# A transformer-and-scan kernel on one NeuronCore: the mixers' projections in matmuls of 256 columns where they were of 512

## The chip, the core and the metric

The kernel runs on one core of one Trainium2 chip. The metric is the time of one execution on the device in microseconds (us). The kernel before takes 1607.89 us in the median of 3 runs (1607.69 to 1608.31). TensorE (PE in the profile, with its weight loads as PEld) multiplies; VectorE (DVE), ScalarE (ACT) and GpSimd (POOL) do the elementwise work; SyncE (SP) issues the loads of weights.

## The reference

256 tokens of width 1024 go through two layers of one block and then one layer of another. Each layer of the first block is a gated feed-forward network, a stage with three mixers, and a second feed-forward network. The part in question is the projection ahead of the mixers:

```
h = rms_norm(x, mix_norm[l])
aq, ak, av, bq, bk, bv, cq, ck, cv, cg, gates = jnp.split(h @ w_in[l], split_points, axis=-1)
```

The first ten pieces of `h @ w_in[l]` are 4608 columns in all: nine groups of 512. The pieces of mixer a (differential attention), b (attention over chunks with a bias table) and c (retention) are made from them; `gates` (3072 columns) scale what the mixers give.

## The kernel before

Every product of two float32 matrices is made from three products of rounded parts: with h = h_hi + h_lo and w = w_hi + w_lo, the kernel adds h_hi·w_hi, h_hi·w_lo and h_lo·w_hi in PSUM. Weights come from HBM in slabs of 128 x 2048 numbers into a ring of five slots. ScalarE writes the high part (`whi`, line 692), then VectorE the low part (`wlo`, line 1913), and only then may TensorE use the slab; TensorE's last matmul of a slab frees the slot (`used`).

Nearly all matmuls have a stationary operand of 128 x 128 and a moving one of 128 x 256. In the feed-forward networks, the gates and the output projections the weights are stationary and the activations move (`block3`, lines 1240 to 1242). In the nine groups (`group(g)`, lines 1438 to 1440) it is the other way round: the activations `h1hi`/`h1lo` (128 of the 1024 features by 128 tokens) are stationary and 512 columns of weights move, so that tokens come out on the partitions. A group takes two slabs, 8 feature blocks k, two halves of the tokens tt and three products: 48 matmuls of 512 columns, each with its own weight load. Two layers of nine groups make 864 such matmuls. tt = 0 and tt = 1 accumulate in two different banks of PSUM, and groups alternate between two pairs of banks.

The order is written out by hand. In each of the two layers TensorE does the last feed-forward products, group 0, the sums over tokens for the norm (`token_sums`, lines 1260 and 1263), groups 1, 2, 3 and 4, and then groups 5 to 8 with the transposes (line 1452) or attention scores (line 1463) of the mixers between them; after group 8 come the gates' products and the rest of the mixers. ScalarE takes each group out of PSUM (line 865). VectorE normalises and rotates the queries and keys (lines 1913, 2232) between its low parts of slabs.

Two terms of the text below: a *restart* is the first matmul of a row of projection, gate or feed-forward matmuls after a wait or after matmuls of another kind; a *train* is all that follow it without a break. The helper `settle` (line 1230) is four small matmuls of 128 x 64 that the program puts into a bank ahead of some of the trains of feed-forward and output matmuls; there is none in the projections.

Of the kernel before, what the change touches and what calls it, by code (L numbers as in the profile page):

```python
# [24 lines left out]
KT = D // P  # L25
S = 256
# [154 lines left out]
def build_program(nc, t):  # L181
# [1036 lines left out]
    def _(pe):  # L1218
        def weights(g):

            slot = PLACE[g] % NS
            pe.wait_ge(lo_done[slot], SPLITS[g])
            return slot
# [13 lines left out]
        def block3(out, slot, b, hi, lo, start, stop, skip=False):  # L1237

            w_hi, w_lo = (w[:, slot, b * P:(b + 1) * P] for w in (whi, wlo))
            pe.matmul(out, w_hi, hi, start=start, stop=False, skip_group_check=skip)  # L1240
            pe.matmul(out, w_lo, hi, start=False, stop=False, skip_group_check=skip)  # L1241
            return pe.matmul(out, w_hi, lo, start=False, stop=stop, skip_group_check=skip)  # L1242
# [11 lines left out]
        def token_sums(n, token_major):  # L1254

            bank = 6 if token_major else 7
            if n == 0:
                pe.wait_ge(first_landed, 16)
            pe.wait_ge(sq_added, n + 1)
            ins = pe.matmul(ps[:, bank, 0:S], ones[:, :], sq[:, 0, :], start=True, stop=True)  # L1260
            if token_major:
                for tt in range(ST):
                    ins = pe.matmul(ps[:, bank, S + tt:S + tt + 1], sq[:, 0, tt * P:(tt + 1) * P], ones[:, 0:1],
                                    start=True, stop=True)
            ins.then_inc(ssum_done, 1)
# [153 lines left out]
        for l in range(DEPTH):  # L1419
# [4 lines left out]
            def group(g):  # L1424

                if g >= 2:
                    pe.wait_ge(proj_evac, NGRP * l + g - 1)
                for half in range(2):
                    slot = weights(m + PROJ0 + 2 * g + half)
                    for kk in range(4):  # L1430
                        k = 4 * half + kk
                        if g == 0 and kk % 2 == 0:
                            pe.wait_ge(h_lo_ready, 4 * (n + 1) + k // 2 + 1)
                        w_hi, w_lo = (w[:, slot, kk * 512:(kk + 1) * 512] for w in (whi, wlo))
                        for tt in range(ST):
                            out = ps[:, 2 * (g % 2) + tt, :]
                            h_hi, h_lo = (h[:, k, tt * P:(tt + 1) * P] for h in (h1hi, h1lo))
                            pe.matmul(out, h_hi, w_hi, start=(k == 0), stop=False)  # L1438
                            pe.matmul(out, h_hi, w_lo, start=False, stop=False)  # L1439
                            ins = pe.matmul(out, h_lo, w_hi, start=False, stop=(k == KT - 1))  # L1440
                    ins.then_inc(used[slot], 1)
                if g == 0:
                    token_sums(n + 1, True)
# [55 lines left out]
            def values(h):  # L1499

                cols = slice(h * P, (h + 1) * P)
                pe.matmul(ps[:, 5, cols], pT[:, 3 * h, :], vA[:, 0, cols], start=True, stop=False)
                pe.matmul(ps[:, 5, cols], pT[:, 3 * h + 1, :], vA[:, 1, cols], start=False, stop=True)
                return pe.matmul(ps[:, 4, cols], pT[:, 3 * h + 2, :], vA[:, 0, cols], start=True, stop=True)

            def b_head(p):

                h = 2 * (p % 4) + p // 4
                return slice(h * HD, (h + 1) * HD)

            def y_b_out(c, par, tt):

                first = 2048 + c * S + tt * P
                return ps_flat[64 * par:64 * par + 64, first:first + P]

            for g in range(5):
                group(g)
# [3 lines left out]
            pe.wait_ge(qk_ready, 3 * l + 1)  # L1521
            transposes(TA, q_and_k(qkA, 4))
            group(5)
            stage(SA1)
            scores(SA1, S)
            group(6)
            stage(SA0)
            scores(SA0, P)
# [11 lines left out]
            for h in range(AH):  # L1540
                ins = values(h)
# [18 lines left out]
            for c in range(4):  # L1560
                for kt in range(2):
                    for par in range(2):
                        p = c + 4 * par
                        pe.matmul(y_b_out(c, par, 1), vB[:, kt, b_head(p)], pT[:, 2 * p + kt, :],
                                  start=(kt == 0), stop=(kt == 1))
# [4 lines left out]
            for c in range(4):  # L1570
                for par in range(2):
                    p = c + 4 * par
                    ins = pe.matmul(y_b_out(c, par, 0), vB[:, 0, b_head(p)], pT[:, p, :], start=True, stop=True)
# [4 lines left out]
            for j in range(2):  # L1578
                for par in range(2):
                    rows = slice(64 * par, 64 * par + 64)  # L1580
                    for kt in range(2):
                        width = S - kt * P
                        ins = pe.matmul(ps[:, 4 + 2 * par + kt, j * width:(j + 1) * width],
                                        qkT[rows, 2 + j, kt * P:(kt + 1) * P],
                                        qkT[rows, j, kt * P:S], start=True, stop=True)
# [3 lines left out]
            for h in range(CH):  # L1589
                cols = slice(h * P, (h + 1) * P)  # L1590
                pe.matmul(ps[:, 4, cols], pTC[:, h, 0, 0:P], vC[:, 0, cols], start=True, stop=True)
                for kt in range(2):
                    ins = pe.matmul(ps[:, 5, cols], pTC[:, h, kt, P:S], vC[:, kt, cols],
                                    start=(kt == 0), stop=(kt == 1))
# [11 lines left out]
            for q in range(6):  # L1606
# [12 lines left out]
                for mm in range(4):  # L1619
                    c = (1 - q % 2) * 1024 + mm * S  # L1620
                    for k in range(4):
                        kk = Y_AT["abc"[q // 2]] + k
                        ins = block3(ps_flat[:, c:c + S], slot, mm * 4 + k, yT_hi[:, kk, :], yT_lo[:, kk, :],
                                     start=(k == 0), stop=(k == 3))
# [35 lines left out]
        def state(d, g, bank, pairs):  # L1660

            for j, (lhs, rhs) in enumerate(pairs):
                ins = pe.matmul(ps[:, bank + 2 * d + g // 2, (g % 2) * S:(g % 2) * S + 192], lhs[:, g * P:(g + 1) * P],
                                rhs[:, g * 192:(g + 1) * 192], start=(j == 0), stop=(j == len(pairs) - 1))
            return ins
# [4 lines left out]
        for d in range(2):  # L1670
            for g in range(NG):
                if (d, g) == (0, 3):
                    pe.wait_ge(sq_added, NF3 + 1)
                    for j in range(2):
                        ins = pe.matmul(ps[:, 0, 0:S], ones[:, :], sq[:, j, :], start=(j == 0), stop=(j == 1))
                    ins.then_inc(sum2_done, 1)
                ins = state(d, g, 4, [(cb_tok[:, i, :], xw_c[i][:, d, :]) for i in range(2)])
# [16 lines left out]
        for j in range(1, 4):  # L1694
# [3 lines left out]
            for c in range(1, 4):  # L1698
                slot = PLACE[b2 + c // 2] % NS
                for k in (2 * j, 2 * j + 1):  # L1700
                    ins = block3(ps[:, c, 0:S], slot, (c % 2) * KT + k, hhi[:, k, :], hlo[:, k, :],
                                 start=False, stop=(k == KT - 1))
# [39 lines left out]
        for c in range(4, 23):  # L1742
            projection(c)
            if c == 4:
                pe.wait_ge(h0_ready, 1)
                for tt in range(ST):
                    ins = pe.matmul(ps[:, 7, 24 * tt:24 * tt + 24], dtT[:, tt * P:(tt + 1) * P], sel[:, 0:24],
                                    start=True, stop=True)
                ins.then_inc(dt_tok_done, 1)
            if c == 8:  # L1750
# [3 lines left out]
                for q, (lhs, rhs) in enumerate(sums):  # L1754
                    ins = pe.matmul(ps[:, 7, 128 + 12 * q:140 + 12 * q], lhs, rhs, start=True, stop=True)
# [5 lines left out]
            if c == 11:  # L1761
# [3 lines left out]
                for e, (lhs, rhs) in enumerate(sums):  # L1765
                    ins = pe.matmul(ps[0:NH, 7, e * P:(e + 1) * P], lhs, rhs, start=True, stop=True)
                ins.then_inc(sums_done, 1)
            if c == 5:
                pe.wait_ge(uz_evac, 2)
                pe.wait_ge(h0_ready, 1)  # L1770
                for tt in range(ST):
                    for ch in range(2):
                        ins = pe.matmul(ps[:, 4 + tt, ch * S:(ch + 1) * S], u_t[:, ch, tt * P:(tt + 1) * P], dft_chan[:, :, :],
                                        start=True, stop=True)
                ins.then_inc(dft_done, 1)
            if c == 7:
                pe.wait_ge(dft_evac, 1)
                for ch in range(2):
                    for tt in range(ST):
                        for part in range(2):  # L1780
                            ins = pe.matmul(ps[:, 6, ch * S:(ch + 1) * S],
                                            w1[:, tt, ch * S + part * P:ch * S + (part + 1) * P], dft_tok[:, tt, part, :],
                                            start=(tt == 0 and part == 0), stop=(tt == 1 and part == 1))
                ins.then_inc(dft_done, 1)
            if c == 20:
# [4 lines left out]
                for d in range(2):  # L1790
                    for g in range(NG):
                        ins = state(d, g, 4, [(b_tok[:, d, :], xw_x[:, d, :])])
# [30 lines left out]
        for tt in range(ST):  # L1823
            for g in range(NG):
                tok = slice(tt * P, (tt + 1) * P)
                ins = pe.matmul(ps[:, 4 + tt, g * P:(g + 1) * P], b_t[:, g, tok], c_t[:, g, tok], start=True, stop=True)
# [65 lines left out]
        for k in (0, 6, 7):  # L1892
# [4 lines left out]
            for tt in range(ST):  # L1897
                ins = pe.matmul(ps[:, 1, tt:tt + 1], sq[:, k, tt * P:(tt + 1) * P], ones[:, 0:1],
                                start=(k == 0 and tt == 0), stop=(k == 7), skip_group_check=True)
# [996 lines left out]
```

## Time and profile before

| | |
|---|---|
| median of 3 runs | 1607.89 us (1607.69 to 1608.31) |
| profiled execution | 1608.59 us |
| span of its trace | 1606.8 us |
| PE busy | 1593.5 us (99%), 13104 matmuls |
| DVE busy | 1291.6 us (80%) |
| ACT busy | 927.2 us (58%) |
| POOL busy | 211.9 us (13%) |
| 864 matmuls of 512 columns (lines 1438 to 1440) | first at 191.6 us, last at 912.1 us of the span, half of them in each layer |

Busy time is the union of an engine's instructions. A matmul's duration in the trace lasts to the end of its results, and the next one starts long before that; what counts is the distance from start to start. Such distances are read from first and last starts and the number of matmuls between them.

### The profile page before, as it was taken

The numbers are of one execution on the slowest core, as the hardware profiler recorded it, in microseconds if no ns is written. First come the engines' busy times: TensorE is split into PE (matmuls) and PEld (weight loads), VectorE is DVE, ScalarE is ACT, GpSimd is POOL, SyncE is SP. The second block draws the span as 40 slices with busy tenths as digits, with TensorE's granted clock in tenths as the row PEclk, the third lists the DMA queues.
The fourth block names the chain that finished last, engine by engine and source line by source line (L and its number), as shares of the span: only waits on it lengthen the run. The fifth ranks groups of instructions, "written<-read, shape, count | busy, mean of one in ns | idle before, by whom it ended". The sixth has DMA issues, their size and how long they took to land.

```text
span 1606.8 us, 29855 instructions
## 1 busy us (share of the span) xinstructions
PE 1593.5 (99%) x13104; PEld 1530.3 (95%) x13104; DVE 1291.6 (80%) x1468; ACT 927.2 (58%) x1113; POOL 211.9 (13%) x125
## 2 busy tenths in 40 slices
PE   9999999999999999999999999999999999999998
PEld 8999988999999999999987899999999989899998
DVE  7887978688888987897878688785899788896655
ACT  7554655685465455554565677464546567754544
POOL 1000100000040001110010000032232378600000
PEclk9999999999999999999999999999999999999999
DMA  7677654444566665766754444555554345335552
GB/s 292 226 271 270 258 188 158 158 146 170 210 217 252 251 257 202 278 243 265 282 187 160 159 155 158 177 218 206 186 207 182 135 151 190 134 132 199 195 186 77
DMA packets 48408, 320.73 MB, mean 200 GB/s; under 512 B 5388, under 2 KB 8204, under 8 KB 10776
## 3 DMA queue, kind: packets, MB, share of 16 engines
q1 hardware_dynamic: 48136, 318.81, 54.0%
q8 instruction: 103, 1.69, 0.4%
q14 instruction: 25, 0.20, 0.0%
q10 hardware_dynamic: 144, 0.02, 0.0%
HBM read 317.74 MB, written 1.07 MB: 198 GB/s over the span
## 4 chain that ended last, share of the span: by engine, by line
PE 91%; DVE 5%; ACT 2%; DMA 1%; issue 0%; SPq 0%; DVEq 0%
PE ps L1240 26%; PE ps L1242 25%; PE ps L1241 25%; PE ps L1438 3%; PE ps L1440 3%; PE ps L1439 3%; DVE wlo L1913 1%; PE ps L1452 1%; ACT whi L692 1%; PE ps L1463 1%; DMA raw<-in_w_dram 1%; PE ps L1725 1%; DVE tmp L1913 1%; DVE qkA L1913 1%; DVE pre L2550 1%
## 5 line engine op out<-in xcount | busy, mean ns | idle before, releaser
L1913 DVE TENSOR_TENSOR wlo<-raw,whi 128x2048 fp32r<-128x2048 f32 (+2 forms) x255 | 583.7, 2297 | 94.3 <-ACT whi L692 90.6
L692 ACT ACTIVATE whi<-raw 128x2048 fp32r<-128x2048 f32 (+1 forms) x264 | 499.9, 1906 | 208.3 <-DMA raw<-in_w_dram 208.0
L1240 PE MATMUL ps<-h1hi,whi 128*128 128x256 f32 x1792 | 500.6, 279 | 1.5 <-DVE wlo L1913 1.5
L1241 PE MATMUL ps<-h1hi,wlo 128*128 128x256 f32 x1792 | 496.6, 277 | 0.0
L1242 PE MATMUL ps<-h1lo,whi 128*128 128x256 f32 x1792 | 496.6, 277 | 0.0
L1240 PEld LDWEIGHTS ps<-h1hi,whi 128*128 128x128 f32 x1792 | 337.8, 189 | 5.4 <-issue 2.3
L1241 PEld LDWEIGHTS ps<-h1hi,wlo 128*128 128x128 f32 x1792 | 337.7, 188 | 0.1
L1242 PEld LDWEIGHTS ps<-h1lo,whi 128*128 128x128 f32 x1792 | 337.4, 188 | 0.0
L1240 PE MATMUL ps<-hid_hi,whi 128*128 128x256 f32 x880 | 243.8, 277 | 0.0
L1242 PE MATMUL ps<-hid_lo,whi 128*128 128x256 f32 x880 | 243.1, 276 | 0.0
L1241 PE MATMUL ps<-hid_hi,wlo 128*128 128x256 f32 x880 | 243.1, 276 | 0.0
L1240 PE MATMUL ps<-hhi,whi 128*128 128x256 f32 x672 | 190.3, 283 | 3.1 <-DVE hlo L2512 1.7
L1242 PE MATMUL ps<-hlo,whi 128*128 128x256 f32 x672 | 186.1, 277 | 0.0
L1241 PE MATMUL ps<-hhi,wlo 128*128 128x256 f32 x672 | 186.1, 277 | 0.0
L1240 PEld LDWEIGHTS ps<-hid_hi,whi 128*128 128x128 f32 x880 | 165.4, 188 | 0.2
L1241 PEld LDWEIGHTS ps<-hid_hi,wlo 128*128 128x128 f32 x880 | 165.2, 188 | 0.0
L1242 PEld LDWEIGHTS ps<-hid_lo,whi 128*128 128x128 f32 x880 | 165.2, 188 | 0.0
L585 POOL TENSOR_TENSOR sq<-sq 128x512 f32<-128x512 f32 x18 | 27.3, 1517 | 927.1 <-ACT sq L721 914.1
L1240 PEld LDWEIGHTS ps<-hhi,whi 128*128 128x128 f32 x672 | 126.4, 188 | 6.5 <-issue 3.2
L1241 PEld LDWEIGHTS ps<-hhi,wlo 128*128 128x128 f32 x672 | 126.3, 188 | 1.3 <-issue 1.2
L1242 PEld LDWEIGHTS ps<-hlo,whi 128*128 128x128 f32 x672 | 126.3, 188 | 0.0
L726 ACT ACTIVATE t_exp<-t_exp 128x512 f32<-128x512 f32 x55 | 34.7, 631 | 139.5 <-DVE t_exp L2067 139.4
(376 smaller groups left out, 2592.6 us busy)
## 6 DMA issues: line engine op xcount, KB each, us to landing
raw<-in_w_dram SPq DMA_DIRECT2D x288, 1024.0 KB, 4.8
from_start<-decay_dram SPq DMA_DIRECT2D x3, 768.0 KB, 4.5
raw<-in_w_dram SPq DMA_DIRECT2D x8, 256.0 KB, 5.8
c_rows<-in_c_rows_dram SPq DMA_DIRECT2D x2, 1024.0 KB, 10.3
relbias<-in_relbias_dram SPq DMA_DIRECT2D x2, 1024.0 KB, 7.8
pv<-in_pv_dram SPq DMA_DIRECT2D x2, 641.0 KB, 7.6
xT<-in_x_dram SPq DMA_DIRECT2D x4, 256.0 KB, 5.0
raw<-in_w_dram SPq DMA_DIRECT2D x2, 512.0 KB, 6.9
```

The costliest lines, as they stand in the source:

```text
L585: step.done(pool.tensor_tensor(sq[:, 0:2, :], sq[:, 0:2, :], sq[:, 2 * j:2 * j + 2, :], ALU.add))
L692: act.activation(whi[:, slot, c], raw[:, slot, c], ACT.Copy).then_inc(hi_done[slot], 1)
L726: step.done(act.activation(v, v, ACT.Exp, scale=-1.0))
L1240: pe.matmul(out, w_hi, hi, start=start, stop=False, skip_group_check=skip)
L1241: pe.matmul(out, w_lo, hi, start=False, stop=False, skip_group_check=skip)
L1242: return pe.matmul(out, w_hi, lo, start=False, stop=stop, skip_group_check=skip)
L1438: pe.matmul(out, h_hi, w_hi, start=(k == 0), stop=False)
L1439: pe.matmul(out, h_hi, w_lo, start=False, stop=False)
L1440: ins = pe.matmul(out, h_lo, w_hi, start=False, stop=(k == KT - 1))
L1452: ins = pe.transpose(ps_flat[:, first + j * P:first + (j + 1) * P], tile, ident[:, :])
L1463: ins = pe.matmul(ps_flat[:, c:c + width], qkT[rows, j, tt * P:(tt + 1) * P], qkT[rows, 4 + j, 0:width], start=True, stop=True)
L1913: return dve.tensor_tensor(out, a, b, op)
```

## The change

Each matmul of 512 moving columns becomes two of 256: for one half of the columns all three products, then for the other half all three. The same stationary operand is therefore loaded six times where it was three. The first matmul of a bank still clears the bank's flags, now once per bank and group, as `start` is set only for the first half.

```diff
-                            pe.matmul(out, h_hi, w_hi, start=(k == 0), stop=False)
-                            pe.matmul(out, h_hi, w_lo, start=False, stop=False)
-                            ins = pe.matmul(out, h_lo, w_hi, start=False, stop=(k == KT - 1))
+                            for n_ in range(2):
+                                c = slice(n_ * S, (n_ + 1) * S)
+                                pe.matmul(out[:, c], h_hi, w_hi[:, c], start=(k == 0 and n_ == 0), stop=False,
+                                          skip_group_check=True)
+                                pe.matmul(out[:, c], h_hi, w_lo[:, c], start=False, stop=False, skip_group_check=True)
+                                ins = pe.matmul(out[:, c], h_lo, w_hi[:, c], start=False, stop=(k == KT - 1),
+                                                skip_group_check=True)
```

The order on TensorE where layer 0 goes from the feed-forward network into group 0, before (hid: its hidden values):

```order
L1240 MATMUL ps<-hid_hi_85,whi 128x256
L1241 MATMUL ps<-hid_hi_85,wlo 128x256
L1242 MATMUL ps<-hid_lo_87,whi 128x256
L1438 MATMUL ps<-whi,h1hi 128x512
L1439 MATMUL ps<-wlo,h1hi 128x512
L1440 MATMUL ps<-whi,h1lo 128x512
```

and in the changed kernel:

```order
L1240 MATMUL ps<-hid_hi_85,whi 128x256
L1241 MATMUL ps<-hid_hi_85,wlo 128x256
L1242 MATMUL ps<-hid_lo_87,whi 128x256
L1440 MATMUL ps<-whi,h1hi 128x256
L1442 MATMUL ps<-wlo,h1hi 128x256
L1443 MATMUL ps<-whi,h1lo 128x256
L1440 MATMUL ps<-whi,h1hi 128x256
L1442 MATMUL ps<-wlo,h1hi 128x256
L1443 MATMUL ps<-whi,h1lo 128x256
```

Three matmuls of 512 have become six of 256 with the same neighbours ahead. The second place, also on TensorE, is the seam between the token sums and group 1, before:

```order
L1440 MATMUL ps<-whi,h1lo 128x512
L1260 MATMUL ps<-sq,ones 128x256
L1263 MATMUL ps<-ones,sq 128x1 x2
L1438 MATMUL ps<-whi,h1hi 128x512
L1439 MATMUL ps<-wlo,h1hi 128x512
L1440 MATMUL ps<-whi,h1lo 128x512
```

and in the changed kernel:

```order
L1443 MATMUL ps<-whi,h1lo 128x256
L1260 MATMUL ps<-sq,ones 128x256
L1263 MATMUL ps<-ones,sq 128x1 x2
L1440 MATMUL ps<-whi,h1hi 128x256
L1442 MATMUL ps<-wlo,h1hi 128x256
L1443 MATMUL ps<-whi,h1lo 128x256
```

Here too only the width and the number of the matmuls differ. No instruction of the other engines is added, removed or moved.

## Rows read from the trace of the kernel before

**Rows 1.** The page: share of the span by engine, granted clock, the last chain.
```profile
PE 1593.5 (99%) x13104; PEld 1530.3 (95%) x13104; DVE 1291.6 (80%) x1468; ACT 927.2 (58%) x1113; POOL 211.9 (13%) x125
...
PEclk9999999999999999999999999999999999999999
...
PE 91%; DVE 5%; ACT 2%; DMA 1%; issue 0%; SPq 0%; DVEq 0%
```

**Rows 2.** One line's matmuls in a stretch: duration min/median/max in ns, first and last start.
```profile
L1438 PE MATMUL ps<-whi,h1hi x47: 394/394/394, 204.2 to 235.8; 128*128 128x512 f32 x47
```

**Rows 3.** Busy us and count (x) by stretch, clock, DMA: first fast, then slow 256-column trains.
```profile
1435.00:1595.00 160.00, 160.00 (x1414) 160.00 (x1414) 99.71 (x90) 79.21 (x73) 0.00 (x0) 1.00 0.47 172
...
1164.50:1185.50 21.00, 21.00 (x181) 21.00 (x180) 19.92 (x30) 10.21 (x12) 5.87 (x2) 1.00 0.56 201
```

**Rows 4.** The same matmul line in six short trains beside or like the projections.
```profile
L1240 PE MATMUL ps<-h1hi,whi x15: 276/276/277, 311.3 to 316.1; 128*128 128x256 f32 x15
L1240 PE MATMUL ps<-h1hi,whi x15: 281/281/281, 346.3 to 351.3; 128*128 128x256 f32 x15
L1240 PE MATMUL ps<-h1hi,whi x31: 276/276/277, 374.9 to 385.1; 128*128 128x256 f32 x31
L1240 PE MATMUL ps<-h1hi,whi x15: 281/281/281, 924.3 to 929.2; 128*128 128x256 f32 x15
L1240 PE MATMUL ps<-h1hi,whi x15: 281/281/281, 1219.2 to 1224.2; 128*128 128x256 f32 x15
L1240 PE MATMUL ps<-hhi,whi x7: 281/281/281, 1291.9 to 1294.0; 128*128 128x256 f32 x7
```

**Rows 5.** PE in order of time (start, duration in us): three seams after narrow matmuls.
```profile
203.03 0.50 PE L1263 MATMUL ps<-ones,sq 128*128 128x1 f32 x4
203.39 0.48 PE L1438 MATMUL ps<-whi,h1hi 128*128 128x512 f32 x1
203.71 0.39 PE L1439 MATMUL ps<-wlo,h1hi 128*128 128x512 f32 x1
...
1218.57 0.37 PE L1322 MATMUL ps<-small,ones 128*128 128x12 f32 x2
1218.80 0.36 PE L1240 MATMUL ps<-h1hi,whi 128*128 128x256 f32 x1
```

**Rows 6.** The chain of waits, 214 to 243 us: start, us, what.
```profile
214.41 0.24 PE ps L1440
214.67 1.27 ACT qkA L865 x2
...
219.72 2.29 DVE wlo L1913
...
240.33 2.30 DVE wlo L1913
```

**Rows 7.** PE in order of time, at the two slabs of group 4.
```profile
236.22 0.40 PE L1440 MATMUL ps<-whi,h1lo 128*128 128x512 f32 x1
236.63 0.47 PE L1438 MATMUL ps<-whi,h1hi 128*128 128x512 f32 x1
236.94 0.40 PE L1439 MATMUL ps<-wlo,h1hi 128*128 128x512 f32 x1
...
241.84 0.40 PE L1439 MATMUL ps<-wlo,h1hi 128*128 128x512 f32 x1
242.08 0.39 PE L1440 MATMUL ps<-whi,h1lo 128*128 128x512 f32 x1
242.68 0.51 PE L1438 MATMUL ps<-whi,h1hi 128*128 128x512 f32 x1 [0.21 <-DVE wlo L1913]
243.02 0.40 PE L1439 MATMUL ps<-wlo,h1hi 128*128 128x512 f32 x1
```

**Rows 8.** Two long pieces of the chain of waits, 243 to 300 us.
```profile
248.47 1.75 PE ps L1452 x16
261.22 1.93 PE ps L1463 x16
```

## The prediction

> **What bounds the kernel now.** I read the page first, then the matmul lines by group, the timeline of TensorE around every restart, and last the chain of waits in the projection stage. On the page TensorE is busy for 99% of the span at the full granted clock of 2.4 GHz (tenths of 9, mean 0.999), and 91% of the chain that ended last is TensorE; no other engine is over 80% [rows 1]. So the time is the sum of start-to-start distances of some 13,000 matmuls, and a change in the distance counts nearly everywhere. The exception to look for is a place where TensorE arrives at a slab before VectorE has finished its low part.
>
> Distances. In a train (all matmuls that follow a restart without a break) of 512 columns line 1438 comes once in three, and 46 intervals take 235.8 − 204.2 = 31.6 us: 31.6 / 138 = 229.0 ns per matmul [rows 2]. The 256-column matmuls have two paces. In the last feed-forward network, 1414 matmuls touch a stretch of 160 us; about 2.4 of them only overlap its edges (each lasts 0.28 us, over two distances), which leaves 160 / 1411.6 = 113.3 ns [rows 3], its first row. In another stretch it is 21 / (181 − 2.4) = 117.6 ns [rows 3], its second; from the first and last starts of several such trains I take 117.8. The reader can tell the paces apart by the duration of one matmul: 276 ns at 113.3, 281 at 117.8, and a train keeps its pace from its restart to its end [rows 4]. The 512-column matmuls have a slow pace as well, but rarely: from 236.94 to 241.84 there are 21 distances, 233.3 ns each [rows 7]. That is one half-group of the 18 half-groups of layer 0, and layer 1 has none.
>
> **The change part by part.** It removes 864 matmuls of 512 columns and 864 weight loads, and adds 1728 of each with 256 columns. What counts is two of the new distances against one old one:
>
> - fast pace: 2 × 113.3 = 226.7 ns (from unrounded thirds of 340 ns), against 229.0: −2.3 ns per pair
> - slow pace: 2 × 117.8 = 235.6 ns: +6.6 ns per pair
>
> These are the two bounds of the unknown, from rows of the same shape in the same program, and they lie on both sides of zero. All 864 pairs fast would be −2.0 us, all slow +5.7 us, before anything is hidden. That loads and matmuls can alternate at 113.3 ns, I need not assume: the feed-forward networks do it for hundreds of us with a load for each matmul, beside VectorE at 62% [rows 3]. The operands are the other way round here (weights move), but both are 128 contiguous and 256 contiguous numbers, and the 512-column trains show no other penalty. The wait instructions, evacuations and DMAs are the same; the last matmul of a slab ends within 0.01 us of where it did. I cost these at nothing.
>
> The Trainium skill has a rule that speaks against the change. "TensorE: Matmul & The Clock Gate", section "Wait — 56ns, not 53.3ns?", gives a matmul a fixed cost of about 2.5 ns on top of N / 2.4 GHz, so 864 more of them would cost 2.2 us. The trace doesn't bear it out: by that rule the two widths would be 109 and 216 ns, and they are 113.3 and 229.0 [rows 2, 3]. The same page says nothing of two paces.
>
> Which pace does each new train get? Each layer has these trains, in matmuls of the old width:
>
> - Group 0 (48) follows the feed-forward products without a break, and these are fast; it stays fast: −0.11 us.
> - Groups 1 to 3 (144) restart after the token sums, whose last matmuls have one column [rows 5]. The nearest things in the trace are two restarts of 256 columns after matmuls of 12 and 24 columns, at 1218.8 and 1291.4; both trains are slow [rows 4, 5]. I take slow: 144 × 6.6 = +0.95 us, a third of it in group 1.
> - Group 4 (2 × 24) restarts twice after a wait for a slab.
> - Groups 5 to 8 (48 each) restart after sixteen transposes or sixteen scores [rows 8]. The gates' products restart after the same kinds: after scores fast at 311.3 and slow at 924.3, after transposes slow at 346.3 and fast at 374.9 [rows 4]. Of the 20 trains from 299 to 376 and 912 to 990 us that no `settle` precedes, I count 8 slow, and of the longer ones after transposes or scores about half. I take two of four slow: 2 × 48 × 6.6 − 2 × 48 × 2.3 = +0.41 us.
>
> What VectorE hides. At 242.68 TensorE waits for a low part [rows 7]. The chain behind it begins where group 1 ends, at 214.41: ScalarE takes group 1 out, squares it, makes a high part, and from 219.72 VectorE works nearly without a break to 242.6 [rows 6]. So group 0 and group 1 move that chain, and groups 2, 3 and 4a lie beside it. TensorE's room there: at 236.22 it waits for 236.63 − 236.22 − 0.23 = 0.18 us, and at 242.08 for 0.60 − 0.23 = 0.37 us; each wait also costs a restart, 0.31 − 0.23 = 0.08 and 0.34 − 0.23 = 0.11 us. Together 0.74 us of cover. Groups 1 to 3 slow and 4a slow (24 × (235.6 − 233.3) = 0.06) ask for 1.01 us, less 0.11 from group 0. So TensorE is late by 0.90 − 0.74 = +0.16 us at the middle of group 4, while the low part is late by 0.32 − 0.11 = 0.21 us: both come within 0.1 us of each other, and I take +0.2. If the waits vanish there is no restart, and group 4b goes on slow: 24 × 6.6 = +0.16. Had the trains been fast, the waits would only grow and the cover give back nothing but groups 0 and 1.
>
> Sum per layer: +0.2 + 0.16 + 0.41 = +0.77 us. Layer 1 has the same waits, the second 0.1 us longer, so +0.7. Together +1.5 us. The profiled execution took 1608.59 us (span 1606.8 and 1.8 around it) and would become 1610.1; it lies 0.7 us above the median of 1607.89, and so my forecast is **1609.4 us**.
>
> **The rivals.**
>
> - *All trains fast.* For it: half of the restarts in the gates are fast, and 13 of the 14 restarts of 512 columns reach their fast pace. Against it: the two slow trains after narrow matmuls. Each layer: −0.11 and −0.11 for groups 0 and 1 (2 and 3 drown in the wait for VectorE), −0.05 for 4b, −0.44 for groups 5 to 8: −0.7, both layers −1.4: 1606.5 us.
> - *All slow, and the later trains thrown anew.* This is the slower side. All of groups 5 to 8 slow gives 0.2 + 0.16 + 4 × 0.32 = 1.6 per layer, +3.2 us. It decides against the kernel when, on top, the fast trains behind the projections that no `settle` protects turn slow, since their restarts now come at other instants: the longest, from 374.5 on and its like in layer 1, have 240 matmuls each at 4.5 ns, +1.1 us apiece [rows 4]. With both: +5.4, 1613.3 us. Against it: those restarts follow the same instructions as before, and the executions of this kernel agree within 0.6 us, so the pace isn't drawn afresh in each execution.
> - *A fixed price for each matmul* (the skill's rule above): +2.2 us, 1610.1 us. Two distances of 113.3 are less than one of 229.0, so the rows leave no room for it. Little chance.
> - *No change at all.* If the cover of 0.74 us took all, and groups 5 to 8 came out even: 1607.9 us. This is the middle between the first rival and my forecast and needs no mechanism of its own.
>
> **How the numbers follow.** My forecast (trains mixed) 0.55, all fast 0.2, mostly or all slow with or without the later trains 0.17, the fixed price 0.03, anything else 0.05. A measurement of this kernel tells about 0.2% (3.2 us) from no change. The mixed case spans about 1607.5 to 1611, since each of its eight undecided groups is worth 0.43 us; with the all-fast end at 1606.5 and the all-slow end at 1611.1 the range is 1606.2 to 1612.0. Slower by over 0.2% needs the second rival nearly in full: 0.14. Faster by over 0.2% is beyond what all 864 pairs could give: 0.03. Within 0.2%: 0.83.
>
> **What would show it.** Lines 1440, 1442 and 1443 of the changed kernel: 276 ns in group 0, 281 in groups 1 to 3, and a mixture in groups 5 to 8; the wait at 236.2 gone and that at 242.1 near zero. From the start of group 0 to the gates' first product each layer should take 0.7 to 0.8 us longer. I am wrong if the new distances are neither 113.3 nor 117.8 (weights as the moving operand would then matter, or six loads of which four repeat), if groups 1 to 3 are fast, or if the difference lies outside the projections.

## The result and the profile after

The changed kernel takes 1612.86 us in the median of 7 executions, the kernel before 1608.20 us in 7 on the same chip: ratio 1.0035, 95% interval 1.0026 to 1.0044. It is slower by some 0.3%; I had forecast 1609.4 us and a range up to 1612.0, so the prediction was wrong: the time lies above the range. Two of the seven executions took 1618 us; they were not profiled, and what they had more is open. One execution of a kernel further down took 1650.04 us at a granted clock of 0.96 and is left out of that kernel's median. The profiled execution took 1612.52 us, with a span of 1610.7.

The page of the changed kernel, against [rows 1]:

```profile
PE 1598.3 (99%) x13968; PEld 1573.0 (98%) x13968; DVE 1295.7 (80%) x1468; ACT 926.9 (58%) x1113; POOL 214.3 (13%) x125
...
PEclk9999999999999999999999999999999999999999
...
PE 96%; DVE 1%; ACT 1%; DMA 0%; SPq 0%; issue 0%; DVEq 0%; ACTq 0%
```

There are 864 more matmuls, each with its load. The clock is the same. VectorE has left the chain (5% before, 1% now): it no longer sets anything in the projections, because TensorE has become later there than VectorE.

The first of the three products of the split groups, by stretch (duration min/median/max in ns, first and last start): group 0, groups 1 to 4, groups 5, 6, 7 and 8 of layer 0, and group 5 of layer 1.

```profile
L1440 PE MATMUL ps<-whi,h1hi x32: 276/276/278, 191.1 to 201.7; 128*128 128x256 f32 x32
...
L1440 PE MATMUL ps<-whi,h1hi x111: 278/280/280, 203.2 to 242.1; 128*128 128x256 f32 x111
...
L1440 PE MATMUL ps<-whi,h1hi x32: 280/280/366, 249.8 to 260.8; 128*128 128x256 f32 x32
L1440 PE MATMUL ps<-whi,h1hi x31: 279/279/387, 263.2 to 273.9; 128*128 128x256 f32 x31
L1440 PE MATMUL ps<-whi,h1hi x31: 279/279/388, 275.8 to 286.5; 128*128 128x256 f32 x31
L1440 PE MATMUL ps<-whi,h1hi x31: 279/279/363, 288.9 to 299.6; 128*128 128x256 f32 x31
...
L1440 PE MATMUL ps<-whi,h1hi x32: 279/279/365, 865.6 to 876.6; 128*128 128x256 f32 x32
```

276 ns means 113.3 ns from start to start, 279 to 281 means 117.8: in the second row 110 intervals of three matmuls take 242.1 − 203.2 = 38.9 us, 117.9 ns each. So group 0 kept the fast pace and every other train of the split groups took the slow one, ten of ten in the two layers (groups 1 to 4 are one train a layer here, groups 5, 6, 7 and 8 one each). In [rows 2] a 512-column matmul took 229.0 ns, two of the new ones now take 235.6.

At the two places where TensorE waited before [rows 7]:

```profile
235.97 0.28 PE L1443 MATMUL ps<-whi,h1lo 128*128 128x256 f32 x1
236.09 0.28 PE L1440 MATMUL ps<-whi,h1hi 128*128 128x256 f32 x1
236.21 0.28 PE L1442 MATMUL ps<-wlo,h1hi 128*128 128x256 f32 x1
...
242.33 0.28 PE L1443 MATMUL ps<-whi,h1lo 128*128 128x256 f32 x1
242.45 0.32 PE L1440 MATMUL ps<-whi,h1hi 128*128 128x256 f32 x1
242.61 0.28 PE L1442 MATMUL ps<-wlo,h1hi 128*128 128x256 f32 x1
```

The first wait is gone, and of the second a distance of 0.16 in place of 0.12 us is left.

From the first projection matmul to the first gates' matmul a layer takes 110.40 us where it took 108.84 (191.61 to 300.45 before, 191.11 to 301.51 after; layer 1 the same within 0.01 us). That is +1.56 us twice. Outside the projections one long train has changed its pace, the gates' and branches' 240 matmuls of layer 0 (line 1240, before at 276 ns in [rows 4]):

```profile
L1240 PE MATMUL ps<-h1hi,whi x29: 281/281/281, 376.0 to 385.9; 128*128 128x256 f32 x29
```

Its 240 matmuls at 4.45 ns give +1.05 us. So: 1.56 + 1.05 + 1.56 = 4.17, less 0.50 us that this execution was ahead already at 20 us of the span, plus 0.25 us at one stop (from the last matmul ahead of it to the restart 0.47 us at 1206 us of the span before, 0.72 us at 1210 us after). That makes 3.9 us; the two spans differ by 3.96. Behind that stop short trains of 24 to 54 matmuls in the second block changed their pace in both directions and about cancel. The first 20 us wait for the first loads, and between the profiles of this study they lie between 1.0 us ahead of and 0.6 us behind the kernel before; that is not the change's.

### The profile page after: what moved, and what is told of

Its sections match the earlier page's. It is cut to its first block, busy times and chain, and to the rows that moved or that the text cites. A ratio compares the mean times of both kernels' runs of the same rounds, so it can differ in the third digit from the quotient of the medians.

```text
span 1610.7 us, 31583 instructions
## 1 busy us (share of the span) xinstructions
PE 1598.3 (99%) x13968; PEld 1573.0 (98%) x13968; DVE 1295.7 (80%) x1468; ACT 926.9 (58%) x1113; POOL 214.3 (13%) x125
## 4 chain that ended last, share of the span: by engine, by line
PE 96%; DVE 1%; ACT 1%; DMA 0%; SPq 0%; issue 0%; DVEq 0%; ACTq 0%
PE ps L1240 26%; PE ps L1241 26%; PE ps L1242 26%; PE ps L1440 4%; PE ps L1442 4%; PE ps L1443 4%; PE ps L1456 1%; PE ps L1467 1%; PE ps L1729 1%; ACT whi L692 0%; DMA raw<-in_w_dram 0%; PE ps L1230 0%; DVE wlo L1917 0%; PE ps L1568 0%; PE ps L1597 0%; PE ps L1785 0%
## 5 line engine op out<-in xcount | busy, mean ns | idle before, releaser
L1440 PE MATMUL ps<-whi,h1hi 128*128 128x256 f32 x576 | 161.8, 281 | 0.0
L1442 PE MATMUL ps<-wlo,h1hi 128*128 128x256 f32 x576 | 160.7, 279 | 0.0
L1443 PE MATMUL ps<-whi,h1lo 128*128 128x256 f32 x576 | 160.6, 279 | 0.0
```

The costliest lines, as they stand in the source:

```text
L1440: pe.matmul(out[:, c], h_hi, w_hi[:, c], start=(k == 0 and n_ == 0), stop=False, skip_group_check=True)
L1442: pe.matmul(out[:, c], h_hi, w_lo[:, c], start=False, stop=False, skip_group_check=True)
L1443: ins = pe.matmul(out[:, c], h_lo, w_hi[:, c], start=False, stop=(k == KT - 1), skip_group_check=True)
```

## The experiments

The table gives each kernel's median with its ratio to the kernel before (and its 95% interval), and the length of the stage from the first projection matmul to the first gates' matmul, layer 0 / layer 1, from the profile.

| kernel | median, us | ratio | stage, us |
|---|---|---|---|
| before | 1608.0 to 1608.6 | 1 | 108.84 / 108.85 |
| changed | 1612.86 | 1.0035 (1.0026 to 1.0044) | 110.40 / 110.41 |
| changed, once more | 1612.78 | 1.0024 (1.0015 to 1.0033) | 110.40 / 110.41 |
| settle ahead of the groups | 1613.23 | 1.0031 (1.0019 to 1.0044) | 111.49 / 111.49 |
| settle ahead of gate slab 10 | 1614.28 | 1.0031 (1.0018 to 1.0045) | 110.83 / 110.40 |
| first feature block wide | 1611.09 | 1.0017 (1.0007 to 1.0027) | 109.91 / 109.91 |
| only groups 5 to 8 split | 1610.42 | 1.0013 (1.0004 to 1.0023) | 110.06 / 110.14 |
| product by product | 1614.06 | 1.0038 (1.0023 to 1.0053) | 110.40 / 110.91 |
| roles exchanged | 1612.12, one execution | | 109.60 / 109.46 |
| switches chosen | 1608.91 | 1.0002 (0.9993 to 1.0011) | 109.00 / 109.00 |
| switch after one more | 1609.48, one execution | | 109.00 / 109.00 |
| switches refitted | 1609.00 | 1.0006 (0.9989 to 1.0024) | 109.00 / 109.01 |

**The changed kernel once more.** Nothing is edited.

> The changed kernel once more. If the pace of a train belongs to the program: the same trains at 281 ns as in its first profile, all of groups 1 to 8 in both layers, and about 1612.9 us. If it is drawn anew in each execution: some of the ten trains fast.

The same ten trains were slow, the train at 376 us too, and both stages had the same length to 0.01 us. In the projections, the gates and the feed-forward networks the pace of a train belongs to the program here; it isn't drawn in each execution. That doesn't hold for every train: two short ones of the second block, of 24 and 48 matmuls, were slow in the first profile of the changed kernel and fast in this one. The longer of them, first and then second profile:

```profile
L1240 PE MATMUL ps<-hhi,whi x16: 281/281/384, 1426.4 to 1431.8; 128*128 128x256 f32 x16
...
L1240 PE MATMUL ps<-hhi,whi x16: 276/276/386, 1426.6 to 1431.8; 128*128 128x256 f32 x16
```

**Only groups 5 to 8 split.** Groups 0 to 4 keep their matmuls of 512 columns.

```diff
+                            if g < 5:
+                                pe.matmul(out, h_hi, w_hi, start=(k == 0), stop=False, skip_group_check=True)
...
+                                continue
```

> Only groups 5 to 8 are split, groups 0 to 4 keep 512 columns. Theory A with the cover by VectorE: each of the four groups costs 48 x 6.4 ns = 0.305 us, 1.22 us a layer, 2.4 us in all, and 1.05 us more if the gates' train at 375 us falls slow again: 1610.7 or 1611.7 us. If the cost of the change sat in groups 1 to 4 instead, under 1609 us.

All eight split trains were slow, and the stages 1.22 and 1.29 us longer; four times 0.305 is 1.22, and in layer 1 TensorE also stopped briefly ahead of group 0. So of the change's 1.56 us a layer, 1.22 lie in groups 5 to 8 and only 0.34 in groups 0 to 4, though those have 240 of the 432 pairs. 192 slow pairs cost 1.22 us where nothing covers them. Groups 1 to 4 would cost 1.2 us by the same price (192 × 6.4 ns); the waits for VectorE, and group 0 with its 0.1 us less, took the rest. This train of 240 matmuls at 376 us was fast again: so the price there (1.05 us) isn't a price of the split as such. Why it is paid in the changed kernel and not here wasn't found.

**Settle ahead of the groups.**

```diff
                     slot = weights(m + PROJ0 + 2 * g + half)
+                    if half == 0 and g in (1, 4, 5, 6, 7, 8):
+                        settle(2 * (g % 2))
```

> The changed kernel with the four small matmuls of settle() ahead of groups 1, 4, 5, 6, 7 and 8. Theory A (the pace is set at a restart; 117.8 ns a matmul after a bad one, 113.3 after a good one): the trains behind a settle show 276 ns a matmul in place of 281. Each group 5 to 8 then gains 95 x 4.45 ns = 0.42 us and pays about 0.19 us for the settle; groups 1 and 4 gain at most 0.2 us, as VectorE takes over. Against the changed kernel about -2.0 to -2.5 us, so about 1610.5 us; against the kernel before +2. Theory B (weights as the moving operand, or six loads with four repeats, cost 4.45 ns by themselves once the matmul is 256 wide): 281 ns stays, and the 12 settles add about 2 us: 1614.9 us.

Neither theory held in full. Groups 1 to 3, the second half of group 4 and group 5 of layer 0, in this kernel:

```profile
L1442 PE MATMUL ps<-whi,h1hi x95: 276/276/384, 203.7 to 235.7; 128*128 128x256 f32 x95
...
L1442 PE MATMUL ps<-whi,h1hi x16: 276/276/384, 242.9 to 248.1; 128*128 128x256 f32 x16
...
L1442 PE MATMUL ps<-whi,h1hi x30: 278/280/392, 250.5 to 260.9; 128*128 128x256 f32 x30
```

The train of groups 1 to 3 became fast, so weights as the moving operand do run at 113.3 ns and theory B falls. But the first half of group 4 and all of groups 5 to 8 stayed slow behind the same small matmuls, in both layers. The second half of group 4 restarted with no settle directly ahead of it and became fast, in both layers too: a restart with the weights moving can be a good one. The stage is 1.09 us longer than in the changed kernel. To the end of group 4 this kernel is 0.29 us ahead of it, two settles included; a wait for VectorE of 0.24 us ahead of group 4 takes part of the gain back. From there on the four settles ahead of groups 5 to 8, which bought nothing, make it 1.38 us longer, 0.35 us each.

**Settle ahead of gate slab 10.**

```diff
-            gate_slab(10)
+            gate_slab(10, True)
```

> The changed kernel with settle() ahead of gate slab 10, the start of the train of 240 matmuls at 375 us (layer 0) and 991 us (layer 1). In the changed kernel's profile that train is slow in layer 0 (281 ns). With the settle it should be fast in both: -1.05 us, and +0.2 us for each settle, so about 0.7 us below the changed kernel, 1612.2. If its pace has nothing to do with the excess: +0.4 us.

A miss: the train stayed slow in layer 0 and turned slow in layer 1, where it had been fast. Line 1240 in layer 0 and layer 1 of this kernel, then in layer 0 a feed-forward train behind a stop at 169.4 us, and group 0 behind that train:

```profile
L1240 PE MATMUL ps<-h1hi,whi x28: 281/281/281, 378.4 to 388.0; 128*128 128x256 f32 x28
...
L1240 PE MATMUL ps<-h1hi,whi x29: 281/281/388, 993.8 to 1003.8; 128*128 128x256 f32 x29
...
L1240 PE MATMUL ps<-h1hi,whi x32: 281/281/359, 169.7 to 180.7; 128*128 128x256 f32 x32
...
L1440 PE MATMUL ps<-whi,h1hi x32: 280/280/282, 192.4 to 203.3; 128*128 128x256 f32 x32
```

The last two rows are no part of the edit. In this one execution TensorE stopped inside a feed-forward network (0.31 us from start to start in place of 0.11; the low part of a slab ended at 169.5, so a late slab is likely). The 192 matmuls behind that kept 117.8 ns, and so did the 96 of group 0, which follow them without a stop. That is why this kernel's stage in layer 0 is 110.83 us and not 110.40. 288 times 4.45 ns are 1.28 us. The profile of the kernel with refitted switches (below) has two such trains, of 240 matmuls at 524 us and 144 at 653 us, where the other kernels are fast. Whether the executions of 1618 us had one wasn't seen.

**Product by product.**

```diff
-                            for n_ in range(2):
...
+                            for j_, (h_, w_) in enumerate(((h_hi, w_hi), (h_hi, w_lo), (h_lo, w_hi))):
+                                for n_ in range(2):
+                                    c = slice(n_ * S, (n_ + 1) * S)
+                                    ins = pe.matmul(out[:, c], h_, w_[:, c], start=(k == 0 and j_ == 0 and n_ == 0),
...
```

> All groups split, but product by product: h_hi w_hi for both halves of the columns, then h_hi w_lo for both, then h_lo w_hi for both. Theory A: the order of the six makes no difference, trains at 276 or 281 ns by their restart, total within 1 us of the changed kernel (1612.9). Theory B in the form that a repeated load of the same stationary tile costs: the same tile now comes four times in a row and then the other twice, which changes the number of changes of tile per six (two in place of four), so the pace moves away from 117.8 ns in all groups, down towards 113.3: 1609.5 us or less.

All trains from group 1 on slow at 279 to 281 ns, the stage of layer 0 the same to 0.01 us. The order of the six, and how often a tile is loaded twice in a row, makes no difference to the slow pace. In layer 1 TensorE waited once for 0.2 us for h1lo inside the seam to group 0, and so group 0 restarted and was slow too, +0.5 us: group 0 takes over the pace of what it follows without a stop, fast or slow, and a stop ends that.

**Roles exchanged.** The other two products are edited alike.

```diff
-                                pe.matmul(out[:, c], h_hi, w_hi[:, c], start=(k == 0 and n_ == 0), stop=False,
+                                pe.matmul(out[:, c], w_hi[:, 0:P], h1hi[:, k, :], start=(k == 0 and n_ == 0), stop=False,
...
```

> The changed kernel with the roles in the projections exchanged: 128 columns of the weights are stationary and 256 tokens of h move, as in the gates (the products are other ones than those wanted, the shapes and counts are the same). If weights as the moving operand make the slow pace likelier, the trains of groups 1 to 8 should now be mixed as in the gates (about 12 of 20 fast). If the restart or the place decides, the six trains of a layer stay at 281 ns.

Groups 5, 6, 7 and 8 of layer 0 and then of layer 1, the first product:

```profile
L1440 PE MATMUL ps<-h1hi,whi x28: 276/276/276, 251.0 to 260.2; 128*128 128x256 f32 x28
L1440 PE MATMUL ps<-h1hi,whi x27: 281/281/281, 264.0 to 273.2; 128*128 128x256 f32 x27
L1440 PE MATMUL ps<-h1hi,whi x28: 281/281/281, 276.3 to 285.8; 128*128 128x256 f32 x28
L1440 PE MATMUL ps<-h1hi,whi x27: 276/276/276, 290.0 to 298.9; 128*128 128x256 f32 x27
...
L1440 PE MATMUL ps<-h1hi,whi x29: 281/281/364, 866.0 to 875.9; 128*128 128x256 f32 x29
L1440 PE MATMUL ps<-h1hi,whi x27: 276/276/276, 879.8 to 888.7; 128*128 128x256 f32 x27
L1440 PE MATMUL ps<-h1hi,whi x27: 276/276/276, 892.0 to 900.8; 128*128 128x256 f32 x27
L1440 PE MATMUL ps<-h1hi,whi x29: 281/281/281, 905.0 to 914.9; 128*128 128x256 f32 x29
```

Four of eight are fast, as in the gates; groups 1 to 3 are slow in both layers. (In layer 1 the second half of group 4 and group 0, which restarted behind a short stop, were fast.) With the roles of the changed kernel the same eight places were slow in every one of its relatives: 32 of 32 in the changed kernel, the product-by-product one, the one with groups 5 to 8 and the one with the gate settled. These are eight places in four nearly equal programs and not 32 independent draws, but at the same places the roles made a difference. So the place and the neighbours alone don't decide. My tally from the gates was taken from matmuls with the other roles, and that is the likely reason why it misled; why the roles matter isn't shown.

**First feature block wide.** The first six matmuls of a train keep 512 columns.

```diff
+                            if k == 0 and g in (1, 4, 5, 6, 7, 8):
+                                pe.matmul(out, h_hi, w_hi, start=(k == 0), stop=False, skip_group_check=True)
...
+                                continue
```

> The changed kernel, but the first feature block of groups 1, 4, 5, 6, 7 and 8 (6 matmuls) keeps its 512 columns, the rest is 256 wide. Theory A: the restart is then that of a 512-column matmul, which reached its fast pace in 13 of 14 cases, and the 256-column matmuls behind it take the fast pace over (276 ns), as group 0 did behind the feed-forward products: about 1608 us, 4.5 below the changed kernel, or 1 us less gain if the gates' train at 375 us stays slow. Theory B: 281 ns for all 256-column matmuls, 1612.5 us.

The trains did not take over a fast pace as such: of the six switches from 512 to 256 columns (in groups 1, 4, 5, 6, 7 and 8) five led to the slow pace and that of group 7 to the fast one, and the same in layer 1. What differs is the last wide matmul. Its duration and that of the 256-column matmuls behind it, for groups 6, 7 and 8 of layer 0:

```profile
L1441 PE MATMUL ps<-whi,h1lo x1: 388/388/388, 265.2 to 265.2; 128*128 128x512 f32 x1
...
L1445 PE MATMUL ps<-whi,h1hi x26: 279/279/279, 265.5 to 274.3; 128*128 128x256 f32 x26
...
L1441 PE MATMUL ps<-whi,h1lo x1: 394/394/394, 277.8 to 277.8; 128*128 128x512 f32 x1
...
L1445 PE MATMUL ps<-whi,h1hi x26: 276/276/276, 278.1 to 286.6; 128*128 128x256 f32 x26
...
L1441 PE MATMUL ps<-whi,h1lo x1: 392/392/392, 290.5 to 290.5; 128*128 128x512 f32 x1
...
L1445 PE MATMUL ps<-whi,h1hi x26: 279/279/279, 291.1 to 299.9; 128*128 128x256 f32 x26
```

The distances of 512 columns are not all 229 ns: behind the first few of a train they go round in 226, 229 and 232, with durations of 388, 392 and 394. By the *step* of a wide matmul I mean the distance from its start to the next start. The fast train began behind the 232.

**Switches chosen**, and **one more.** The place of the switch is a table of the number of further wide matmuls:

```diff
+                            products = ((h_hi, w_hi), (h_hi, w_lo), (h_lo, w_hi))
+                            wide = 3 if g == 4 or (g > 0 and g != 2 and g != 3 and k == 0) else (
+                                {1: 1, 5: 1, 6: 2, 7: 0, 8: 1}.get(g, 0) if k == 1 and tt == 0 else 0)
```

> Groups 0 to 3 and 5 to 8 split, group 4 wide. Each train of split groups begins with 512-column matmuls: the first feature block (6 matmuls) and then 1, 1, 2, 0 and 1 more for groups 1, 5, 6, 7 and 8. Theory C: behind a restart the 512-column distances run through a fixed cycle of 226, 229 and 232 ns, and the first 256-column matmul takes the fast pace if it follows the step of 232 and the slow one if it follows 226 or 229. The widened beginnings make every train switch behind a step of 232, so all 256-column matmuls of the projections show 276 ns, in both layers; about -0.55 us a layer against the kernel before, 1607.0 us in all (or +1 us if a gates' train of 240 turns slow). Theory A, in which the pace after any restart is a matter of chance or fixed for all trains in groups 5 to 8: they stay at 281 ns and the time is near the kernel with the first feature block wide (1611).

> As the kernel with chosen switches, but exactly one more wide matmul after the first feature block in groups 1, 5, 6, 7 and 8. Theory C: groups 1 to 3, 5 and 8 fast (276 ns), groups 6 and 7 slow (281 ns), the same in both layers. Theory A: no such pattern.

Which groups would be fast I got only partly right: with chosen switches groups 1 to 3, 6 and 8 (not 5 and 7), with one more groups 1 to 3, 7 and 8 (not 5; 6 slow as expected), alike in both layers. The first steps behind a restart shifted with the edit, so that group 5 switched behind 388 and not behind 394. But each train did what its own last wide matmul says. Group 5 and group 8 with chosen switches:

```profile
L1442 PE MATMUL ps<-whi,h1hi x1: 388/388/388, 251.6 to 251.6; 128*128 128x512 f32 x1
...
L1448 PE MATMUL ps<-whi,h1hi x24: 279/279/279, 252.2 to 260.4; 128*128 128x256 f32 x24
...
L1442 PE MATMUL ps<-whi,h1hi x1: 394/394/394, 290.2 to 290.2; 128*128 128x512 f32 x1
...
L1448 PE MATMUL ps<-whi,h1hi x24: 276/276/276, 290.9 to 298.7; 128*128 128x256 f32 x24
```

**Switches refitted.** The table is {1: 1, 5: 3, 6: 2, 7: 1, 8: 1}.

> As the kernel with chosen switches, but with 3 more wide matmuls in group 5 (it had 1) and 1 more in group 7 (it had none), after the steps that the two runs with switches showed: in both, every one of the ten trains took the fast pace behind a step of 231 or 232 ns and the slow one behind 226 or 229. Theory C: all five trains of each layer now fast (276 ns); against the kernel with chosen switches two groups a layer gain about 0.38 us each, -1.5 us, so about 1607.4 us, 0.5 to 1 us below the kernel before. If the steps behind a restart shift with the new beginning, group 5 or 7 stays at 281 ns.

Not all trains became fast: groups 6 and 7 of layer 0 and 5 and 7 of layer 1 were slow, as their last wide steps were 226 or 229. Over the four kernels with a switch there are 42 switches from 512 to 256 columns inside a train: all 20 behind a step of 231 or 232 ns are fast, all 22 behind 225 to 230 slow. The last step tells the pace without exception, also where an edit moved the switch by a matmul or two in the same group; whether it brings the pace about, or both follow from something else, isn't shown. Choosing it by a count ahead of time failed, since the steps right behind a restart move with small edits. The two that were timed, with chosen and with refitted switches, are even with the kernel before (ratios 1.0002 and 1.0006, both intervals hold 1). The two slow trains of a stage cost some 0.36 us each (80 × 4.45 ns), so with every train fast I estimate 109.0 − 0.7 = 108.3 us, 0.6 less than before; no kernel got there, and none beats the kernel before.

## Why the prediction was wrong

The mechanism was right. Two terms of the sum were wrong: that of groups 5 to 8 was mis-sized, and that of the later trains was put at nothing.

- *Two paces, and their price.* Right: 276 ns and 279 to 281 ns, 113.3 and 117.8 ns from start to start, nothing else. +6.4 ns for a slow pair from groups 5 to 8 against 6.6 forecast.
- *Group 0 fast, −0.1 us a layer.* Right.
- *Groups 1 to 3 slow.* Right, but from two restarts behind narrow matmuls in [rows 4, 5], which have the other roles of the operands. The same kind of inference failed for groups 5 to 8, so some luck is in it.
- *The cover of VectorE.* Right: both waits of [rows 7] are gone or nearly so, and from group 0 to the start of group 5 a layer takes 0.34 us more, where the sum had 0.2 + 0.16.
- *"I take two of four slow" for groups 5 to 8.* Here it failed first: four of four, in both layers. That is 1.22 us a layer in place of 0.41, +1.6 us in all. The tally behind it came from gates, where the weights are stationary. With the weights moving none of the eight trains was fast in any of four kernels; with the roles exchanged half were. A row of the same shape and with the same kind of neighbours wasn't a row of the same case: the operands had the other roles, I had seen it, and I had waved it through.
- *The later trains.* The sum had nothing for them. The rival had them, and one of its two came: +1.05 us in layer 0. I gave it little, since the restart followed the same instructions. It was slow in both profiles of the changed kernel; in eight of the other kernels it was fast again, and in one slow in both layers. Why is open.
- *What each does to the time.* With 1.6 us more for groups 5 to 8 the forecast would have been 1611.0 us, inside the range; with 1.05 us more for the later train 1612.1 us, just outside it. Another 0.3 us is that the kernel before took 1608.20 us in this comparison, where I had counted from 1607.89. The remaining 0.5 us isn't assigned; the profile has 0.25 us of it at one stop.
- *The rival that came true* was the second, without half of its last term: all slow and one train thrown, which by its own numbers is 1607.9 + 3.2 + 1.1 = 1612.2 us, against 1612.86 measured. The range ended 0.9 us below it, because I took the limit of the projections alone for the end of the range.
- *The fixed price for each matmul.* Group 0 of the changed kernel has 96 matmuls at 113.3 ns in place of 48 at 229.0, and was 0.1 us shorter. A fixed price for 48 more matmuls would have made it longer. It is excluded here. The price of that rival was the Trainium skill's ("TensorE: Matmul & The Clock Gate", section "Wait — 56ns, not 53.3ns?"), about 2.5 ns on top of N / 2.4 GHz; this trace doesn't agree, with 113.3 and 229.0 ns where it gives 109 and 216.

## What to carry to other kernels

Where TensorE is the bound, read the start-to-start distance in each train, not a mean over the kernel: here the same matmul has two stable paces, 4% apart, and splitting a 512-column matmul trades a width that came back to its fast pace after 13 of 14 restarts for one that was slow behind all ten of its restarts and stayed so until the next stop. A pace taken from matmuls of the same shape is a bound, not a forecast, until it comes from the same roles of the operands and the same kind of restart. And a few idle tenths of a microsecond on the bounding engine hide a loss ahead of them, but not the same loss where there are none.

## What the runs showed of the hardware

- A train of loads and 256-column matmuls holds one of two paces from its restart to the next stop: 113.3 ns for up to 1488 matmuls, 117.8 ns for up to 337; trains of 512 columns mostly run at 229.0 in steps of 226, 229 and 232 ns, seldom at 233.3 (the first half of group 4 in layer 0 of the kernel before). The granted clock was the full 2.4 GHz in all of them.
- Entering 256 columns from 512 without a stop, the fast pace followed a step of 231 or 232 ns and the slow one any other (225 to 230 ns), 42 of 42.
- The small matmuls of `settle` ahead of a train (four calls, eight matmuls in the trace) don't ensure the fast pace: one of six settled places in the projections became fast at its restart, and a settled train of the gates turned slow.
- What sets the pace at a restart was not found. In slow and in fast trains alike each load starts 2 to 4 ns after a matmul. But the first distance behind a restart goes closely with the pace. Over the twelve traces, in 256-column trains of over 20 matmuls, it was 206 or 207 ns in 85, all of them fast, and 223 ns in 115, all fast; at 224 to 228 ns 37 of 42 were slow, at 201 ns 92 of 113. The same places recur in these counts from kernel to kernel.
